# Two transformer blocks on one core: the low halves of a projection's input made by GpSimd in place of VectorE

## The chip, the cores and the metric

The kernel runs on one core of a Trainium2 chip. The metric is the device time of one execution in microseconds; the median of three runs is given. "TensorE", "VectorE", "ScalarE", "GpSimd" and "SyncE" are PE, DVE, ACT, POOL and SP in the profile.

## The reference

The input is x of 512 tokens by 1024 features. It goes through a first block (an RMS norm, an input projection, a mixer of sparse, convolutional, stick-breaking and dilated attention, group norms, an output projection, an RMS norm and a gated feed-forward) and then through four layers of a second kind. Each of these four is

```python
h = x * (1 + scale[0]) + shift[0]
y = mixer(h, w_in, ..., w_out)      # mLSTM, sliding window, HGRN2, differential attention
x = layer_norm(alpha * x + (1 + gate[0]) * y, ln_g[i, 0], ln_b[i, 0])
h = x * (1 + scale[1]) + shift[1]
y = (silu(h @ w_gate) * (h @ w_up)) @ w_down
x = layer_norm(alpha * x + (1 + gate[1]) * y, ln_g[i, 1], ln_b[i, 1])
```

All is fp32. What matters here are the matrix products h @ w. The kernel splits both factors in a high part, rounded to the engine's fast fp32r format, and a low part, the difference, and adds three products: hi x hi, hi x lo and lo x hi.

## The kernel before, in words

**Layout.** x lies in SBUF as eight chunks of 128 features by 512 tokens (`x[:, c, :]`). A product's input stands in `h_hi` and `h_lo`, eight chunks each. It comes from `h_tmp` (norms) or from `proj` (a mixer's output); there is one pair `h_hi`, `h_lo` for all of them.

**Weights.** They stream as 501 slots of 128 x 1024 through a ring of four (`RING`). SyncE loads a slot in `raw`, ScalarE copies it to `w_hi` (line 1187), GpSimd subtracts and writes `w_lo` (line 568), TensorE multiplies and counts `slot_used`, which lets ScalarE make the slot four further on. Four slots are always prepared ahead.

**Hand-over.** At each of 15 places a new input is produced while TensorE already starts on it: 5 in front of an input projection (the first block, layers 0 to 3), 5 in front of an output projection, 5 in front of a feed-forward. There TensorE runs `early_chunk(c)` for c = 0 to 7 on the first three slots (`EARLY`): it waits for `part_hi` of the chunk, does six matmuls on `h_hi`, waits for `part_lo`, and does three on `h_lo` (lines 753, 754, 758). Behind the eighth chunk the three slots are given free together; TensorE still has the fourth, prepared slot, some 5.4 us of work (24 matmuls, lines 665 to 667).

**Who makes the input.** ScalarE writes `h_hi` (line 1219, or 1266 with the scale and shift of a layer norm). VectorE writes `h_lo = value - h_hi` (`low`, line 1572). In a layer norm VectorE does, for each chunk, `times` (line 1617, x times a bank) and `less` (line 1621, x minus a bank); ScalarE then writes `h_hi` (1266) and `h_tmp` (1268), and VectorE subtracts (1572). ScalarE afterwards scales x eight times (line 1272), and goes on with its own program: in a feed-forward a Silu (line 1463, with a table load), then `w_hi` of the next slots. VectorE's order in this place is fixed by the code: `less(c)` stands behind the low half of an earlier chunk.

**Around it.** In the input projections of layers 1 and 3 VectorE copies finished banks to `proj` (line 1664). After the fourth tile it makes the rope tables (lines 1928 to 1941: on `rope_t`, no bank), and only afterwards the next copies; TensorE has four banks to fill meanwhile. GpSimd, beside `w_lo`, loads the positions for them (line 631) and, in layer 1, clears `swa_k` and `swa_v`.

**Queues.** Every engine runs its instructions in the order of its program; between engines there are semaphores. GpSimd's program before is `low_to(...)`, a loop over weight slots, with the first block's convolution, the DMA of positions, two memsets and parts of two mixers between.

Of the kernel before, what the change touches and what calls it, by code (L numbers as in the profile page):

```python
# [8 lines left out]
F32 = mybir.dt.float32  # L9
# [3 lines left out]
ALU = mybir.AluOpType  # L13
# [13 lines left out]
LEAD = 4  # L27
# [179 lines left out]
def stream_length(parts):  # L207
    n = 0
    for part in parts:
        tiles, values = IN_PROJ[part]  # L210
        n += len(tiles) + len(values) + n_gates(part) + (8 if part == "first" else 0) + DT + 2 * FT + 3 * DT
    return n


def program(nc, xT, wstream, ada, cond, cols, kept, bigc, layerc, pos, yT, parts):
    slots_total = stream_length(parts)
    ctx = ExitStack()
    with ctx:
# [345 lines left out]
        @block.gpsimd  # L564
        def _(pool):
            def low(k, i=0, step=0):
                pool.wait_ge(sm.hi_done, k + 1 + step * i)
                nc.gpsimd.tensor_tensor(w_lo[k % RING][:, :, :], raw[k % RING][:, :, :],  # L568
                                        w_hi[k % RING][:, :, :].bitcast(F32), ALU.subtract).then_inc(sm.lo_done, 1)

            def low_to(end):

                k, count = n["slot"], end - n["slot"]
                if count >= RING:
                    with loop(pool, count // RING) as i:
                        for q in range(RING):
                            low(k + q, i, RING)
                for q in range(count // RING * RING, count):
                    low(k + q)
                n.add(slot=count)  # L580

            def hgrn():

                pool.wait_ge(sm.hg_ready, 1)
                for s, step in enumerate(HG_STEPS):
                    for hd, lv in step:
                        if lv < 2:
                            continue
                        b = HG_WIDTH[lv - 1]
                        pool.wait_ge(sm.hg_mm, HG_MM[hd, lv - 1])  # L590
                        early, factor = halves(hg_k[:, hd, :], b)[0], hg_factor(hd, b, 1)
                        if lv == 9:
                            early, factor = early[:, 0:1, :], factor[:, 0:1, :]
                        nc.gpsimd.tensor_tensor(early, early, factor, ALU.mult).then_inc(sm.hg_early, 1)
                    if s in HG_LOW:
                        low(n["slot"])
                        n.add(slot=1)

            n = Counts()
            def gated_convolution():  # L600

                g = nc.gpsimd
                steps = 0

                def link(ins):

                    nonlocal steps
                    steps += 1
                    ins.then_inc(sm.conv_step, 1)
                    pool.wait_ge(sm.conv_step, steps)  # L610

                pool.wait_ge(sm.lin_free, len(IN_PROJ["first"][0]))
                for t in range(2):
                    u, y, w = proj[:, 13 + t, :], proj[:, 11 + t, :], [col("conv_w", 3 * t + i) for i in range(3)]
                    link(g.tensor_tensor(u, u, y, ALU.mult))
                    link(g.tensor_scalar(y, u, w[2], None, ALU.mult))
                    for lag in (1, 2):
                        link(g.tensor_scalar(conv_tmp[:, lag:S], u[:, 0:S - lag], w[2 - lag], None, ALU.mult))
                        link(g.tensor_tensor(y[:, lag:S], y[:, lag:S], conv_tmp[:, lag:S], ALU.add))
                    link(g.tensor_tensor(proj[:, 2 + t, :], y, proj[:, 2 + t, :], ALU.mult))  # L620

            first_slot = 0
            for at, part in enumerate(parts):
                tiles, values = IN_PROJ[part]
                if part == "first":
                    low_to(len(tiles) + len(values) + 8 + LEAD)
                    gated_convolution()
                if part in (1, 3):
                    low_to(first_slot + LEAD)
                    pool.wait_ge(sm.lin_free, lin_total(parts[:at]))  # L630
                    pool.dma_start(rope_i[:, :], pos).then_inc(sm.pos_loaded, 16)
                if part == 3:
                    low_to(first_slot + len(tiles) + len(values) + LEAD)
                    for hd in range(8):
                        pool.wait_ge(sm.rope_out, len(SWA_TILES) + 8 + hd + 1)
                        k = proj[:, 8 + hd, :]
                        nc.gpsimd.tensor_scalar(df_k[:, hd, :], k, block64[:, HD:HD + 1], float(HD), ALU.mult,
                                                ALU.mult).then_inc(sm.df_moved, 1)
                        pool.wait_ge(sm.df_moved, hd + 1)
                        nc.gpsimd.tensor_scalar(k, k, block64[:, 0:1], float(HD), ALU.mult,  # L640
                                                ALU.mult).then_inc(sm.df_keys, 1)
                if part == 1:
                    low_to(first_slot + LEAD + 2)
                    nc.gpsimd.memset(swa_k[:, :, :, :], 0.0)
                    op = nc.gpsimd.memset(swa_v[:, :, :, :, :], 0.0)
                    op.then_inc(sm.swa_zero, 1)
                if part == 2:
                    low_to(first_slot + len(tiles) + len(values) + LEAD)
                    hgrn()
                first_slot += stream_length([part])  # L650
            low_to(slots_total)

# [905 lines left out]
        def _(dve):  # L1558
# [25 lines left out]
                op.then_inc(sm.n_inv, 1)  # L1584
                dve.wait_ge(sm.n_spread, n["root"])

            def rms_input(gain):
                root()
                for c in range(DT + 1):
                    if c < DT:  # L1590
                        v.scalar_tensor_tensor(h_tmp[:, c, :], x[:, c, :], col(gain, c), inverse_root, ALU.mult,
                                               ALU.mult).then_inc(sm.h_ready, 1)
                    if c:
                        low(c - 1, h_tmp[:, c - 1, :])
                n.add(h=DT)

            def modulated_input(layer):

                for c in range(DT + 1):
                    if c:  # L1600
                        low(c - 1, h_tmp[:, c - 1, :])
                    if c < DT:
                        v.tensor_scalar(h_tmp[:, c, :], x[:, c, :], mod_col(layer, 0, ONE_SCALE, c),
                                        mod_col(layer, 0, SHIFT, c), ALU.mult, ALU.add).then_inc(sm.h_ready, 1)
                n.add(h=DT)

            def ln_columns(layer, sub, gain_at):

# [14 lines left out]
            def layer_norm(split):  # L1623
# [9 lines left out]
                dve.wait_ge(sm.ln_inv, 2 * n["ln"] - 1)  # L1633
                v.scalar_tensor_tensor(ln_drop, ln_mean, 1.0 / D, ln_rstd, ALU.mult, ALU.mult).then_inc(sm.ln_inv, 1)

                def part_low(c):
                    if split:
                        dve.wait_ge(sm.h_ready, n["h"] + c + 1)
                        low(c, h_tmp[:, c, :])

                dve.wait_ge(sm.ln_spread, 2 * n["ln"] - 1)
                for c in range(DT):
                    times(c)
                    if c == 0:
                        dve.wait_ge(sm.ln_spread, 2 * n["ln"])
                    if c == 1:
                        part_low(0)
                    less(c)
                    if c > 1:
                        part_low(c - 1)  # L1650
                part_low(DT - 1)
                n.add(h=DT if split else 0)

            def tile_done(slots):

# [112 lines left out]

            def group_norms(items):

                done = 0
                group_inverse(0)
                for t in range(len(items) + 1):
                    if t == 2 and len(items) > 4:
                        group_inverse(1)
                    if t < len(items):
                        group_norm(items, t, (4, 5))
                    if t:
                        for _ in items[t - 1]["src"]:
                            low(done, proj[:, done, :])  # L1780
                            done += 1
                n.add(gn=len(items))

            def attention(jobs, bufs):
                a, g = n["att"], n["att_g"]
# [379 lines left out]
            for at, part in enumerate(parts):  # L2165
# [1 line left out]
                layer = None if part == "first" else part  # L2167
                n.add(lc=2 if part == "first" else 1)
                if part == "first":
                    rms_input("g_mix")  # L2170
# [34 lines left out]
                if out_norms(part):  # L2205
                    group_norms(out_norms(part))
                else:
                    for c in range(DT):
                        low(c, proj[:, c, :])
                ahead = parts[at + 1] if at + 1 < len(parts) else None  # L2210
                if part == "first":
                    add_residual(1)
                    rms_input("g_ffn")
                    ffn(ahead, layer)
                    add_residual(3)
                else:
# [115 lines left out]
```

## Time and profile before

| what | value |
|---|---|
| time, median of 3 runs | 3532.15 us (3524.84 to 3534.9) |
| span of the profiled execution (its own time outside the span is not listed) | 3519.8 us |
| busy: TensorE / VectorE / ScalarE / GpSimd | 94% / 48% / 35% / 37% |
| mean granted TensorE clock | 0.964 of full speed |
| `w_lo` on GpSimd (line 568) | 501 x 2449 ns |
| `w_hi` on ScalarE (line 1187) | 501 x 1057 ns |
| DMA | 376.09 MB, 107 GB/s on average |

A line of the timeline gives the start in us, the duration in us, the engine, the line of the kernel, the operation, output<-inputs, the shape and how many instructions are merged in it. In brackets stands how long the engine was idle before, and which instruction of which engine ended that. A matmul's listed duration reaches past the start of the next one, since they are pipelined.

### The profile page before, as it was taken

The page shows a single profiled execution, that of the slowest core. Times are in us where ns is not written, and L with a number is a line of the kernel's source. Part 1 is how long each engine was busy: PE and PEld are TensorE (multiplying, and loading weights), DVE is VectorE, ACT ScalarE, POOL GpSimd, SP SyncE. Part 2 cuts the span into 40 slices and gives each one's busy share as a digit, 9 for nine tenths or more (in the row PEclk, how much of TensorE's full clock was granted, in tenths as well). Part 3 has the DMA queues.
Part 4 walks back from the last instruction along what each step waited for, and adds up shares of the span by engine and source line. Part 5 has one row for each costly group of instructions (what it writes and reads, how often), then busy time and mean ns, then how long its engine had stood idle before and what let it go on. Part 6 is the DMA issues. An engine that isn't in the chain of part 4 may idle for free.

```text
span 3519.8 us, 42555 instructions
## 1 busy us (share of the span) xinstructions
PE 3325.5 (94%) x14988; PEld 2629.1 (75%) x14988; DVE 1691.7 (48%) x2835; ACT 1230.2 (35%) x1914; POOL 1312.6 (37%) x603
## 2 busy tenths in 40 slices
PE   7987899999989999989999999999999998999998
PEld 6755578886757888767788878767888775678886
DVE  2344545512246554477655333666653447662223
ACT  3246433322335332336532243125332422643322
POOL 3430144443313444331444444533444343034442
PEclk9978999999999999989999999999999998999998
DMA  4310045532213554220455333103554231023331
GB/s 143 102 42 1 25 148 195 206 115 89 78 42 103 203 195 156 93 66 19 146 196 203 125 96 95 37 31 107 203 191 155 93 102 43 1 61 107 95 102 66
DMA packets 103105, 376.09 MB, mean 107 GB/s; under 512 B 11456, under 2 KB 11584, under 8 KB 102848
## 3 DMA queue, kind: packets, MB, share of 16 engines
q1 hardware_dynamic: 102816, 373.86, 32.0%
q8 instruction: 80, 1.31, 0.2%
q14 instruction: 49, 0.40, 0.0%
q0 software_dynamic: 160, 0.52, 0.0%
HBM read 372.24 MB, written 2.10 MB: 106 GB/s over the span
## 4 chain that ended last, share of the span: by engine, by line
PE 51%; issue 36%; POOL 10%; DVE 1%; ACT 1%; DMA 0%; POOLq 0%; SPq 0%; DVEq 0%; ACTq 0%
PE bank L665 14%; PE bank L667 14%; PE bank L666 14%; POOL w_lo L568 9%; PE bank L1096 1%; PE bank L709 1%; PE bank L710 1%; PE bank L711 1%; PE bank L1065 0%; PE bank L753 0%; PE bank L754 0%; PE bank L758 0%; PE bank L1003 0%; PE bank L1005 0%; PE bank L1004 0%
## 5 line engine op out<-in xcount | busy, mean ns | idle before, releaser
L568 POOL TENSOR_TENSOR w_lo<-raw,w_hi 128x1024 fp32r<-128x1024 f32 x501 | 1224.3, 2449 | 2100.7 <-ACT w_hi L1187 2100.7
L1187 ACT ACTIVATE w_hi<-raw 128x1024 fp32r<-128x1024 f32 x501 | 526.1, 1057 | 1234.8 <-PE bank L667 1021.2
L665 PE MATMUL bank<-h_hi,w_hi 128*128 128x512 f32 x2264 | 885.8, 391 | 12.0 <-DVE proj L1664 6.2
L666 PE MATMUL bank<-h_lo,w_hi 128*128 128x512 f32 x2264 | 882.5, 390 | 0.0
L667 PE MATMUL bank<-h_hi,w_lo 128*128 128x512 f32 x2264 | 882.1, 390 | 0.0
L665 PEld LDWEIGHTS bank<-h_hi,w_hi 128*128 128x128 f32 x2264 | 425.9, 188 | 106.0 <-POOL w_lo L568 8.2
L666 PEld LDWEIGHTS bank<-h_lo,w_hi 128*128 128x128 f32 x2264 | 426.0, 188 | 89.0 <-issue 1.0
L667 PEld LDWEIGHTS bank<-h_hi,w_lo 128*128 128x128 f32 x2264 | 426.0, 188 | 88.8
L2120 DVE CUSTOM_DVE_ANT_0 ada_raw<-ada_raw,cond_row 128x1024 f32<-128x1024 f32 x192 | 307.4, 1604 | 272.9 <-DMA ada_raw<-ada 263.1
L665 PE MATMUL bank<-hid_hi,w_hi 128*128 128x512 f32 x880 | 344.0, 391 | 0.0
L667 PE MATMUL bank<-hid_hi,w_lo 128*128 128x512 f32 x880 | 342.4, 389 | 0.0
L666 PE MATMUL bank<-hid_lo,w_hi 128*128 128x512 f32 x880 | 342.4, 389 | 0.0
L2136 DVE TENSOR_TENSOR hid_lo<-layer_const,hid_hi 128x512 f32 (+1 forms) x110 | 222.0, 2018 | 108.3 <-ACT hid_hi L1468 108.3
L1703 DVE SCALAR_TENSOR_TENSOR x<-bank,mod,x 128x512 f32<-128x512 f32 x64 | 48.0, 750 | 304.8 <-PE bank L667 294.7
L666 PEld LDWEIGHTS bank<-hid_lo,w_hi 128*128 128x128 f32 x880 | 165.2, 188 | 35.2 <-issue 1.0
L665 PEld LDWEIGHTS bank<-hid_hi,w_hi 128*128 128x128 f32 x880 | 165.2, 188 | 35.0 <-issue 1.0
L667 PEld LDWEIGHTS bank<-hid_hi,w_lo 128*128 128x128 f32 x880 | 165.2, 188 | 34.4
L1463 ACT ACTIVATE layer_const<-bank 128x512 f32<-128x512 f32 x110 | 65.6, 597 | 317.6 <-PE bank L667 308.5
L753 PE MATMUL bank<-h_hi,w_hi 128*128 128x512 f32 x360 | 154.7, 430 | 17.8 <-ACT h_hi L1266 11.5
L2133 DVE TENSOR_TENSOR layer_const<-bank,layer_const 128x512 f32<-128x512 f32 x110 | 75.9, 690 | 192.6 <-PE bank L667 163.2
L754 PE MATMUL bank<-h_hi,w_lo 128*128 128x512 f32 x360 | 149.9, 416 | 0.0
L1664 DVE COPY proj<-bank 128x512 f32<-128x512 f32 x68 | 45.5, 689 | 214.9 <-PE bank L667 204.1
(343 smaller groups left out, 4123.1 us busy)
## 6 DMA issues: line engine op xcount, KB each, us to landing
raw<-weights SPq DMA_DIRECT2D x501, 512.0 KB, 3.5
ada_raw<-ada SPq DMA_DIRECT2D x192, 512.0 KB, 4.3
layer_const<-layer_const SPq DMA_DIRECT2D x5, 512.0 KB, 4.4
x<-x_t SPq DMA_DIRECT2D x1, 2048.0 KB, 7.6
cond_row<-cond SPq DMA_DIRECT2D x4, 512.0 KB, 4.4
y_t<-x SPq DMA_DIRECT2D x8, 256.0 KB, 2.0
tables<-big_const SPq DMA_DIRECT2D x1, 768.0 KB, 7.5
cols<-columns SPq DMA_DIRECT2D x1, 569.5 KB, 8.6
```

The lines of the kernel that those rows point to most:

```text
L568: nc.gpsimd.tensor_tensor(w_lo[k % RING][:, :, :], raw[k % RING][:, :, :], w_hi[k % RING][:, :, :].bitcast(F32), ALU.subtract).then_inc(sm ...
L665: mm(out, w_hi[r][:, at, :], hi, start=first and at == 0, stop=False)
L666: mm(out, w_hi[r][:, at, :], lo, start=False, stop=False)
L667: op = mm(out, w_lo[r][:, at, :], hi, start=False, stop=last and at == len(pairs) - 1)
L753: mm(out, w_hi[r][:, c, :], h_hi[:, c, :], start=c == 0, stop=False)
L754: mm(out, w_lo[r][:, c, :], h_hi[:, c, :], start=False, stop=False)
L1187: fn(w_hi[t % RING][:, :, :], raw[t % RING][:, :, :], ACT.Copy).then_inc(sm.hi_done, 1)
L1463: fn(sil[q % 2], bank[(mt + 2 * q) % 4][:, :], ACT.Silu).then_inc(sm.sil_done, 1)
L1703: op = v.scalar_tensor_tensor(x[:, m, :], b[:, :], mod_col(layer, sub, ONE_GATE, m), x[:, m, :], ALU.mult, ALU.add)
L2120: v.tensor_tensor_reduce(w, w, cond_row[:, :], 1.0, 0.0, ALU.mult, ALU.add, ada_part[:, kc:kc + 1]).then_inc(sm.ada_used, 1)
L2133: v.tensor_tensor(sil[q % 2], bank[(mt + 2 * q + 1) % 4][:, :], sil[q % 2], ALU.mult).then_inc(sm.lin_free, 2)
L2136: v.tensor_tensor(hid_lo[:, q + 4 * i, :], sil[q % 2], hid_hi[:, q + 4 * i, :].bitcast(F32), ALU.subtract).then_inc(sm.part_lo, 1)
```

## The change

GpSimd gets a function `input_low` with the subtraction, which waits for `h_ready` (h_tmp is written, where it comes from a norm) and for `part_hi`. It is called in each part of the program in front of the input projection (but for the first), of the output projection and of the feed-forward. VectorE's low halves go in the same places; `part_lo` is now counted up by GpSimd there, and by VectorE in the first hand-over and for the feed-forward's hidden values.

```diff
+            def input_low(tile, scaled):
+                for c in range(DT):
+                    if scaled:
+                        pool.wait_ge(sm.h_ready, n["h"] + c + 1)
+                    pool.wait_ge(sm.part_hi, n["part"] + c + 1)
+                    nc.gpsimd.tensor_tensor(h_lo[:, c, :], tile(c), h_hi[:, c, :].bitcast(F32),
+                                            ALU.subtract).then_inc(sm.part_lo, 1)
+                n.add(part=DT, h=DT if scaled else 0)
...
                 if part == "first":
-                    low_to(len(tiles) + len(values) + 8 + LEAD)
+                    n.add(part=DT, h=DT)
+                    low_to(inputs + LEAD)
                     gated_convolution()
+                else:
+                    low_to(first_slot + LEAD)
+                    input_low(lambda c: h_tmp[:, c, :], True)
                 if part in (1, 3):
-                    low_to(first_slot + LEAD)
                     pool.wait_ge(sm.lin_free, lin_total(parts[:at]))
                     pool.dma_start(rope_i[:, :], pos).then_inc(sm.pos_loaded, 16)
...
+                low_to(first_slot + inputs + LEAD)
+                input_low(lambda c: proj[:, c, :], False)
+                low_to(first_slot + inputs + DT + LEAD)
+                input_low(lambda c: h_tmp[:, c, :], True)
+                n.add(part=FT)
...
             def modulated_input(layer):
-                for c in range(DT + 1):
-                    if c:
-                        low(c - 1, h_tmp[:, c - 1, :])
-                    if c < DT:
-                        v.tensor_scalar(h_tmp[:, c, :], x[:, c, :], ...).then_inc(sm.h_ready, 1)
+                for c in range(DT):
+                    v.tensor_scalar(h_tmp[:, c, :], x[:, c, :], ...).then_inc(sm.h_ready, 1)
...
                 for c in range(DT):
                     times(c)
                     if c == 0:
                         dve.wait_ge(sm.ln_spread, 2 * n["ln"])
-                    if c == 1:
-                        part_low(0)
                     less(c)
-                    if c > 1:
-                        part_low(c - 1)
-                part_low(DT - 1)
```

The same lines go from the group norms, from `rms_input` in front of the first block's feed-forward, and from the end of layer 1's mixer.

On VectorE, a layer norm in front of a feed-forward (`L1617` is `times`, `L1621` is `less`, `L1572` the low half, from the first chunk), before:

```order
618 L1617 TENSOR_TENSOR x<-x,bank 128x512
619 L1621 TENSOR_TENSOR x<-x,bank 128x512
620 L1617 TENSOR_TENSOR x<-x,bank 128x512
621 L1572 TENSOR_TENSOR h_lo<-h_tmp,h_hi 128x512
622 L1621 TENSOR_TENSOR x<-x,bank 128x512
623 L1617 TENSOR_TENSOR x<-x,bank 128x512
624 L1621 TENSOR_TENSOR x<-x,bank 128x512
625 L1572 TENSOR_TENSOR h_lo<-h_tmp,h_hi 128x512
```

The same place now (`L1633` is `times`, `L1637` is `less`):

```order
575 L1633 TENSOR_TENSOR x<-x,bank 128x512
576 L1637 TENSOR_TENSOR x<-x,bank 128x512
577 L1633 TENSOR_TENSOR x<-x,bank 128x512
578 L1637 TENSOR_TENSOR x<-x,bank 128x512
579 L1633 TENSOR_TENSOR x<-x,bank 128x512
```

`less` of the second chunk stood behind a low half, which itself stood behind `h_tmp` of ScalarE; now it follows `times` at once.

On GpSimd, the input projection of layer 1 (the loop above is the weight slots of layer 0; the slots' buffers have numbers), before:

```order
44 L568 TENSOR_TENSOR w_lo_64<-raw_56,w_hi_60 128x1024
45 L195 REGISTER_ALU
46 L195 COMPARE_AND_BRANCH
47 L631 DMA rope_i<-positions 128x512
48 L568 TENSOR_TENSOR w_lo_65<-raw_57,w_hi_61 128x1024
49 L568 TENSOR_TENSOR w_lo_62<-raw_54,w_hi_58 128x1024
50 L644 MEMSET swa_k 128x2048
51 L645 MEMSET swa_v 128x2048
```

The same place now:

```order
93 L568 TENSOR_TENSOR w_lo_64<-raw_56,w_hi_60 128x1024
94 L195 REGISTER_ALU
95 L195 COMPARE_AND_BRANCH
96 L605 TENSOR_TENSOR h_lo<-h_tmp,h_hi 128x512 x8
97 L645 DMA rope_i<-positions 128x512
98 L568 TENSOR_TENSOR w_lo_65<-raw_57,w_hi_61 128x1024
99 L568 TENSOR_TENSOR w_lo_62<-raw_54,w_hi_58 128x1024
100 L658 MEMSET swa_k 128x2048
101 L659 MEMSET swa_v 128x2048
```

Eight subtractions stand between the last weight slot that is prepared ahead and the DMA of the positions; the two slots and the memsets behind follow in the same order.

## Rows read from the trace of the kernel before

**Rows 1.** The page, its first line.

```profile
span 3519.8 us, 42555 instructions
```

**Rows 2.** Groups of instructions by shape: xcount | busy us, mean ns | idle before.

```profile
L1572 DVE TENSOR_TENSOR h_lo<-h_tmp,h_hi 128x512 fp32r<-128x512 f32 x80 | 56.4, 706 | 21.5 <-ACT h_tmp L1268 15.7 <-ACT h_hi L1219 5.6
...
L568 POOL TENSOR_TENSOR w_lo<-raw,w_hi 128x1024 fp32r<-128x1024 f32 x501 | 1224.3, 2449 | 2100.7 <-ACT w_hi L1187 2100.7
...
L615 POOL TENSOR_TENSOR proj<-proj 128x512 f32<-128x512 f32 x2 | 2.5, 1264 | 0.1
```

**Rows 3.** Waits of TensorE: waiter <- releaser: us in total, times, longest us.

```profile
PE bank L665 <- DVE proj L1664: 6.2, 2, 5.6
...
PE bank L665 <- POOL w_lo L568: 5.8, 5, 1.7
```

**Rows 4.** Timeline of ScalarE, layer norm in front of layer 1.

```profile
1477.17 0.81 ACT L1266 ACTIVATE h_hi<-x,ln_cols 128x512 fp32r<-128x512 f32 x1 [2.05 <-DVE x L1621]
...
1480.04 0.81 ACT L1266 ACTIVATE h_hi<-x,ln_cols 128x512 fp32r<-128x512 f32 x1 [1.36 <-DVE x L1621]
...
1481.47 0.80 ACT L1266 ACTIVATE h_hi<-x,ln_cols 128x512 fp32r<-128x512 f32 x1
...
1491.33 0.82 ACT L1266 ACTIVATE h_hi<-x,ln_cols 128x512 fp32r<-128x512 f32 x1 [0.40 <-DVE x L1621]
```

**Rows 5.** The same place on VectorE.

```profile
1478.72 0.69 DVE L1572 TENSOR_TENSOR h_lo<-h_tmp,h_hi 128x512 fp32r<-128x512 f32 x1 [0.99 <-ACT h_tmp L1268]
1479.33 0.68 DVE L1621 TENSOR_TENSOR x<-x,bank 128x512 f32<-128x512 f32 x1
```

**Rows 6.** The same place on TensorE: chunk 0, chunks 6 and 7.

```profile
1480.76 1.48 PE L758 MATMUL bank<-h_lo,w_hi 128*128 128x512 f32 x3
...
1494.45 0.84 PE L758 MATMUL bank<-h_lo,w_hi 128*128 128x512 f32 x3
...
1496.49 0.84 PE L758 MATMUL bank<-h_lo,w_hi 128*128 128x512 f32 x3
```

**Rows 7.** Timeline in front of the feed-forward of layer 0, ScalarE and TensorE.

```profile
1120.52 5.75 ACT L1272 ACTIVATE x<-x,ln_cols 128x512 f32<-128x512 f32 x8
...
1131.64 0.50 PE L665 MATMUL bank<-h_hi,w_hi 128*128 128x512 f32 x1 [1.04 <-POOL w_lo L568]
```

**Rows 8.** Timeline in front of the first block's feed-forward, ScalarE and TensorE.

```profile
473.00 1.28 ACT L1463 ACT_TABLE_LOAD   x1
...
482.91 0.84 PE L758 MATMUL bank<-h_lo,w_hi 128*128 128x512 f32 x3
483.33 0.60 ACT L1463 ACTIVATE layer_const<-bank 128x512 f32<-128x512 f32 x1 [9.04 <-PE bank L758]
```

**Rows 9.** Timeline of layer 1's rope tables: ScalarE, VectorE, GpSimd.

```profile
1498.40 1.04 ACT L1187 ACTIVATE w_hi<-raw 128x1024 fp32r<-128x1024 f32 x1
...
1507.76 10.21 POOL L568 TENSOR_TENSOR w_lo<-raw,w_hi 128x1024 fp32r<-128x1024 f32 x4
...
1513.69 1.06 ACT L1187 ACTIVATE w_hi<-raw 128x1024 fp32r<-128x1024 f32 x1 [4.38 <-PE bank L667]
...
1515.76 2.50 DVE L1935 TENSOR_SCALAR rope_t<-rope_t 128x512 f32<-128x512 f32 x1
...
1525.70 2.34 POOL L568 TENSOR_TENSOR w_lo<-raw,w_hi 128x1024 fp32r<-128x1024 f32 x1 [3.01 <-ACT w_hi L1187]
1525.72 2.88 DVE L1938 SCALAR_TENSOR_TENSOR rope_t<-rope_t,rope_t 128x512 f32<-128x512 f32 x1
...
1529.09 0.43 DVE L1941 TENSOR_SCALAR rope_t<-rope_t 128x512 f32<-128x512 f32 x1
```

**Rows 10.** Busy time by stretch; the number behind POOL's is the granted TensorE clock.

```profile
1530.20:1534.60 4.40, 4.40 (x10) 3.43 (x11) 1.71 (x3) 0.00 (x0) 0.00 (x0) 0.50 0.19 78
```

**Rows 11.** Timeline in front of layer 0, VectorE and TensorE.

```profile
828.47 2.09 DVE L1572 TENSOR_TENSOR h_lo<-h_tmp,h_hi 128x512 fp32r<-128x512 f32 x1 [0.70 <-ACT h_hi L1219]
...
830.62 0.96 PE L758 MATMUL bank<-h_lo,w_hi 128*128 128x512 f32 x3 [0.47 <-DVE h_lo L1572]
```

**Rows 12.** The page, costliest groups: VectorE in the feed-forwards.

```profile
L2136 DVE TENSOR_TENSOR hid_lo<-layer_const,hid_hi 128x512 f32 (+1 forms) x110 | 222.0, 2018 | 108.3 <-ACT hid_hi L1468 108.3
...
L2133 DVE TENSOR_TENSOR layer_const<-bank,layer_const 128x512 f32<-128x512 f32 x110 | 75.9, 690 | 192.6 <-PE bank L667 163.2 <-ACT layer_const L1463 29.4
```

More of the change, by code:

```diff
@@ L624, in _ @@
                 tiles, values = IN_PROJ[part]
+                inputs = len(tiles) + len(values) + n_gates(part) + (8 if part == "first" else 0)
                 if part == "first":
-                    low_to(len(tiles) + len(values) + 8 + LEAD)
+                    n.add(part=DT, h=DT)
+                    low_to(inputs + LEAD)
                     gated_convolution()
+                else:
+                    low_to(first_slot + LEAD)
+                    input_low(lambda c: h_tmp[:, c, :], True)
                 if part in (1, 3):
-                    low_to(first_slot + LEAD)
                     pool.wait_ge(sm.lin_free, lin_total(parts[:at]))
@@ L1585, in root, with rms_input @@
                 dve.wait_ge(sm.n_spread, n["root"])
-            def rms_input(gain):
+            def rms_input(gain, split):
                 root()
@@ L1592, in rms_input @@
                                                ALU.mult).then_inc(sm.h_ready, 1)
-                    if c:
+                    if c and split:
                         low(c - 1, h_tmp[:, c - 1, :])
-                n.add(h=DT)
+                n.add(h=DT, part=0 if split else DT)
             def modulated_input(layer):
-                for c in range(DT + 1):
-                    if c:
-                        low(c - 1, h_tmp[:, c - 1, :])
-                    if c < DT:
-                        v.tensor_scalar(h_tmp[:, c, :], x[:, c, :], mod_col(layer, 0, ONE_SCALE, c),
-                                        mod_col(layer, 0, SHIFT, c), ALU.mult, ALU.add).then_inc(sm.h_ready, 1)
-                n.add(h=DT)
+                for c in range(DT):
+                    v.tensor_scalar(h_tmp[:, c, :], x[:, c, :], mod_col(layer, 0, ONE_SCALE, c),
+                                    mod_col(layer, 0, SHIFT, c), ALU.mult, ALU.add).then_inc(sm.h_ready, 1)
+                n.add(h=DT, part=DT)
             def ln_columns(layer, sub, gain_at):
@@ L1634, in layer_norm @@
                 v.scalar_tensor_tensor(ln_drop, ln_mean, 1.0 / D, ln_rstd, ALU.mult, ALU.mult).then_inc(sm.ln_inv, 1)
[L1636 to L1639, printed above, removed]
                 dve.wait_ge(sm.ln_spread, 2 * n["ln"] - 1)
@@ L1645, in layer_norm @@
                         dve.wait_ge(sm.ln_spread, 2 * n["ln"])
-                    if c == 1:
-                        part_low(0)
                     less(c)
-                    if c > 1:
-                        part_low(c - 1)
-                part_low(DT - 1)
-                n.add(h=DT if split else 0)
+                n.add(h=DT if split else 0, part=DT if split else 0)
             def tile_done(slots):
@@ L1769, in group_norms @@
             def group_norms(items):
-                done = 0
                 group_inverse(0)
-                for t in range(len(items) + 1):
+                for t in range(len(items)):
                     if t == 2 and len(items) > 4:
                         group_inverse(1)
[L1776 to L1782, printed above, removed]
+                    group_norm(items, t, (4, 5))
+                n.add(gn=len(items), part=DT)
             def attention(jobs, bufs):
@@ L2169, in _ @@
                 if part == "first":
-                    rms_input("g_mix")
+                    rms_input("g_mix", True)
                     dve.wait_ge(sm.gate_in, 1)
@@ L2207, in _ @@
                 else:
-                    for c in range(DT):
-                        low(c, proj[:, c, :])
+                    n.add(part=DT)
                 ahead = parts[at + 1] if at + 1 < len(parts) else None
@@ L2212, in _ @@
                     add_residual(1)
-                    rms_input("g_ffn")
+                    rms_input("g_ffn", False)
                     ffn(ahead, layer)
```

## The prediction

> **What bounds the kernel now.** I read the page first: TensorE is busy 94% of a span of 3519.8 us (the table above and [rows 1]). An engine that full can only win at places where it waits, so the second view is the list of waits of TensorE [rows 3]. Two of its entries touch the work that the change moves. TensorE waits 5.8 us in five places for `w_lo`, the low half of a weight slot that GpSimd makes (the longest 1.7), and 6.2 us in two places for VectorE to copy a bank to `proj` (5.6 and 0.6). The third view is the timeline of a hand-over from a layer norm to the next projection; the prediction is made there. The change touches 14 of the kernel's 15 hand-overs: 5 in front of an output projection, 5 in front of a feed-forward, 4 in front of an input projection. The very first keeps VectorE.
>
> **What is added and removed.** 14 x 8 = 112 subtractions leave VectorE and go to GpSimd. On VectorE one takes 706 ns; GpSimd has no such row, but a product of the same shape, two SBUF inputs and one output, took 1264 ns there [rows 2]. So VectorE loses 112 x 0.69 = 77 us and GpSimd gains 112 x 1.26 = 142 us. Neither is a time of the kernel. What counts is whether TensorE asks for `h_lo` before GpSimd has it, and who else is freed.
>
> **Can GpSimd keep up?** In a hand-over TensorE does nine matmuls per chunk; at full clock a chunk takes 1496.49 - 1494.45 = 2.04 us [rows 6]. GpSimd needs about 1.3, so after chunk 0 it stays ahead. Chunk 0 of a layer norm: ScalarE starts h_hi at 1477.17, and h_tmp is finished when VectorE starts its subtraction, at 1478.72 [rows 4, 5]. GpSimd would finish at 1478.72 + 0.05 + 1.26 = 1480.03; TensorE reached the matmuls on h_lo at 1480.76 [rows 6]. All seven layer-norm hand-overs have this shape: no cost. Bounds for an unseen operation: at 1.26 nothing, and at 2.45 (a whole weight slot, twice the size [rows 2]) each chunk would be 0.4 late. I take 1.26, the row of the same shape and kind. In front of output projections the spread matmuls lengthen TensorE's chunk, so there is more room.
>
> **Term 1: ScalarE comes free earlier.** VectorE runs two operations on x, then one low half, per chunk; ScalarE writes h_hi and h_tmp per chunk. ScalarE's own step, with VectorE not in its way, is 1481.47 - 1480.04 = 1.43 us per chunk [rows 4]. But it waited 1.36 us for VectorE before chunk 1, since VectorE stood idle 0.99 us at the low half of chunk 0 and did `less(1)` only afterwards (1479.33) [rows 4, 5]. Without the low halves VectorE needs about 1.32 per chunk (two operations of 0.68, the second waiting for the first), less than 1.43, so ScalarE becomes the slower of the two and still beats TensorE's 2.04. ScalarE then finishes its 16 writes at 1477.17 + 8 x 1.43 = 1488.6; before, the last pair began at 1491.33 and ended at 1492.8 [rows 4], so it is 4.1 us earlier. Behind them stand eight scalings of x (5.75 [rows 7]), in a feed-forward a table load (1.28 [rows 8]), a Silu, and only then the next weight's high half. In front of the feed-forward of layer 0 VectorE's delay so reached TensorE: it idled 1.04 us for `w_lo` and went on at 1131.64 [rows 7]. In front of the feed-forward of the first block, where ScalarE is not late, the table load ran ten microseconds ahead (473.00), and the Silu began at 483.33, 0.42 after TensorE started its last three early matmuls (482.91) [rows 8]. With 4.1 us back ScalarE is in that situation behind all seven layer norms that feed a projection. The longest wait was 1.7, so all five disappear: 5.8 us. A listed idle understates the loss, because a matmul is listed with 0.39 but the next begins 0.23 later; that adds 0.16 each. Sum 5.8 + 5 x 0.16 = 6.6 us.
>
> **Term 2: the rope tables.** In the input projection of layer 1 ScalarE began `w_hi` at 1498.40; not late, it would begin at 1496.49 + 0.42 = 1496.9 [rows 6, 8, 9]. GpSimd's work behind it (two weight slots, two memsets, four weight slots, a block without a gap) moves 1.4 us earlier with it, while VectorE's tables start when the fourth tile is done, as before. VectorE's operations there, on `rope_t` alone, are stretched by GpSimd: L1935 took 2.50 beside `w_lo`, and an operation of the same form, L1941, 0.43 alone, and L1938 took 2.88 because `w_lo` began at 1525.70, 0.02 before it [rows 9]. The Trainium skill says why ("SBUF — State Buffer", section "SBUF: two separate sides"): the port pair that the two engines share is locked for a whole instruction. Worked through with these durations: the four slots at 1507.76 took 10.21, so 2.55 each; three of them now end at about 1514.0, while the fourth needs a `w_hi` that ends at 1513.69 + 1.06 = 1514.75. In that gap L1935 goes through at 1514.3 in 0.43, where it began at 1515.76 and took 2.50. What follows keeps a lead of 0.8 to 2 us, L1938 is then no longer caught by the `w_lo` at 1525.70, and the last operation, L1941, starts 0.1 to 0.4 us ahead of it. VectorE then comes to the banks at about 1525.9 in place of 1529.09 + 0.43 = 1529.5, 3.6 us earlier. TensorE had restarted at half its clock, granted 0.50 for 4.4 us [rows 10], after 5.6 us of idleness; with 2 us idle I expect it to keep the clock, as it did behind the idle 1.04 at 1131.64, whose matmul is listed with 0.50 (at half clock three take 1.48 [rows 6], over 0.6 for one), and that is 4.4/2 = 2.2 more. Sum 5.8. If the last operation just misses the gap, only 1.1 is left of it. In layer 3 the same tables cost 0.6; this goes too, with its 0.16: 0.8.
>
> **Term 3: a loss in front of layer 0.** Here h_tmp comes from VectorE, and GpSimd is busy with a weight slot. VectorE's subtraction was held by it (2.09 in place of 0.69, so until about 829.9) and TensorE waited 0.47 [rows 11]. Now GpSimd can start chunk 0 at 830.1 to 830.6, the later time if VectorE's waiting modulation goes first, and ends at 831.4 to 831.9, against 828.47 + 2.09 = 830.56. TensorE is 0.8 to 1.3 later on h_lo; some of that comes back at chunk 1, where it waited for a high half that is now early. I take +0.5 us, between a full return (0) and none (1.3).
>
> **Others, at nothing.** The positions' DMA on GpSimd's queue moves behind eight subtractions; it then leaves at about 1488.6 + 1.3 = 1490, more than 10 us before the tables. In normed products VectorE's two-SBUF operations share the lock with GpSimd; there are two such hand-overs, layers 0 and 2, at worst one held step each, 2 x 1.26 = 2.5; I take nothing, since TensorE's spread matmuls give room. VectorE enters the feed-forward early and its condition products meet GpSimd's last chunks; chunk 7 would be ready at 1490 and is asked for at 1496.49, so they may be held for 6 us. GpSimd's weight slots are not delayed: its next one needs banks that TensorE frees only after the last chunk. If that cover failed, each slot would cost at most its 2.45.
>
> **Sum.** -6.6 - 5.8 - 0.8 + 0.5 = -12.7 us: the profiled span would be 3507.1. Only the span of that execution is shown, and the runs' median lies 12.35 above it; against the median, 3532.15 - 12.7 = 3519.5.
>
> **Rivals.** (A) The gap in the tables is missed. Phases of 0.1 us decide it, and the trace of before cannot. Sum -12.7 + 4.7 = -8: 3524. (B) Nothing measurable: ScalarE's lateness has another source. For it speaks that the freed engine is busy only 48% of the span; against it the 0.40 that ScalarE idled for VectorE before a later h_hi of a layer norm [rows 4]. With terms 1 and 2 at nothing the time is 3530 to 3533. The Trainium skill ("Perfetto Trace Analysis", section "Optimizing Scalar/DVE Operations") warns that moving work between these two engines "might not help". The stretched rows agree with its reason, but only for operations without a bank: in the feed-forward, beside the same weight slots, L2136 (two SBUF inputs) averages 2018 ns and L2133 (a bank and SBUF) 690 [rows 12]. The operations of a layer norm read a bank, as L2133 does. (C) Slower: GpSimd does not keep up. Its place is each chunk after the first; it decides from a step of 2.04 us. For it speak the 1264 against 706 ns, and the lock with products and modulations. At a step of 2.3 (1.26, plus waits, plus one held operation of VectorE each) TensorE loses 14 x 7 x 0.26 = 25 us, net +17 after term 1: 3549. Against it: only three hand-overs have such VectorE operations at all.
>
> **From cases to numbers.** A measurement of this kernel can tell 0.3%, 10.6 us, from no change. Forecast 0.50, A 0.22, B 0.18, C 0.10. The forecast passes 10.6 by little, so of its 0.50 I count 0.40 as faster and 0.10 as same; of A 0.06 is faster, 0.16 same. Together: faster 0.46, same 0.10 + 0.16 + 0.18 = 0.44, slower 0.10. Range 3513 to 3532: it holds the forecast, A and most of B.
>
> **What would show it.** Right: no wait of TensorE for `w_lo` behind a layer norm; `w_lo` starting about 1 us behind the early matmuls there; ScalarE writing h_hi every 1.43 us; GpSimd's `h_lo` at about 1.26; the wait of 5.6 down to about 2, without a stretch at clock 0.50 behind it. Wrong: waits of the h_lo matmuls on GpSimd beyond layer 0; a GpSimd step over 2 us; a rope wait of 4 us or more.

## The result, and the profile after

The changed kernel takes 3510.43 us (median of 4 runs, 3505.9 to 3514.07); the kernel before, beside it, 3530.91 (4 runs). The ratio is 0.9945, 95% interval 0.9933 to 0.9956. A second comparison, experiment e5 below, gave 0.9951 (0.9937 to 0.9964), with 24 runs of before at a median of 3528.92. By these two ratios the change saves 17.3 to 19.4 us. The forecast was 3519.5, with a range from 3513 to 3532: the direction was right, the forecast was 9.1 us too high, and the measured time lies 2.6 us below the range.

The page of the changed kernel, two lines, answering to [rows 1]:

```profile
span 3506.9 us, 42581 instructions
...
PE 3323.4 (95%) x14988; PEld 2627.9 (75%) x14988; DVE 1642.4 (47%) x2723; ACT 1226.1 (35%) x1914; POOL 1467.7 (42%) x715
```

The forecast for this span was 3507.1. That it was met almost exactly is partly luck, as will be seen.

The waits of TensorE on `proj`, answering to [rows 3]. There is no row for `w_lo` any more:

```profile
PE bank L684 <- DVE proj L1670: 2.0, 1, 2.0
```

GpSimd's new instructions by shape (xcount: shortest/median/longest ns, first and last start), answering to [rows 2]:

```profile
L605 POOL TENSOR_TENSOR h_lo<-h_tmp,h_hi x72: 1280/1297/2348, 465.0 to 3135.7; 128x512 fp32r<-128x512 f32 x72
L605 POOL TENSOR_TENSOR h_lo<-proj,h_hi x40: 1261/1287/1789, 402.6 to 3084.8; 128x512 fp32r<-128x512 f32 x40
```

I had taken 1.26. The layer norm in front of layer 1, ScalarE (four of its lines) and then GpSimd, answering to [rows 4]:

```profile
1477.86 0.81 ACT L1285 ACTIVATE h_hi<-x,ln_cols 128x512 fp32r<-128x512 f32 x1 [2.05 <-DVE x L1637]
...
1479.29 0.80 ACT L1285 ACTIVATE h_hi<-x,ln_cols 128x512 fp32r<-128x512 f32 x1
...
1487.76 0.80 ACT L1285 ACTIVATE h_hi<-x,ln_cols 128x512 fp32r<-128x512 f32 x1
...
1489.17 5.75 ACT L1291 ACTIVATE x<-x,ln_cols 128x512 f32<-128x512 f32 x8
```

```profile
1479.46 11.19 POOL L605 TENSOR_TENSOR h_lo<-h_tmp,h_hi 128x512 fp32r<-128x512 f32 x8 [1.22 <-ACT h_tmp L1287]
```

Before, ScalarE's scaling of x in this place:

```profile
1492.75 5.75 ACT L1272 ACTIVATE x<-x,ln_cols 128x512 f32<-128x512 f32 x8
```

From the first h_hi to the first scaling of x ScalarE now takes 11.31 us; before it was 1492.75 - 1477.17 = 15.58. The eight steps are 1.41 us each, with no wait for VectorE. GpSimd's eight take 1.40 each, as fast as ScalarE feeds them. In front of the feed-forward of layer 0, whose early matmuls end at 1127.1, answering to [rows 7] (ScalarE, then GpSimd):

```profile
1126.70 0.60 ACT L1482 ACTIVATE layer_const<-bank 128x512 f32<-128x512 f32 x1 [0.16 <-PE bank L777]
```

```profile
1128.33 5.22 POOL L568 TENSOR_TENSOR w_lo<-raw,w_hi 128x1024 fp32r<-128x1024 f32 x2 [5.72 <-ACT w_hi L1206]
```

The Silu now waits for TensorE and not TensorE for the weight. `w_lo` starts 1.2 us behind the early matmuls in all four feed-forwards behind a layer norm, where it started 4.0 to 4.7 behind them.

The rope tables, answering to [rows 9, 10]: VectorE, TensorE, and the busy time of two stretches.

```profile
1514.84 0.43 DVE L1935 TENSOR_SCALAR rope_t<-rope_t 128x512 f32<-128x512 f32 x1
...
1518.83 0.69 DVE L1938 SCALAR_TENSOR_TENSOR rope_t<-rope_t,rope_t 128x512 f32<-128x512 f32 x1
...
1525.99 0.43 DVE L1941 TENSOR_SCALAR rope_t<-rope_t 128x512 f32<-128x512 f32 x1
```

```profile
1527.08 0.50 PE L684 MATMUL bank<-h_hi,w_hi 128*128 128x512 f32 x1 [1.96 <-DVE proj L1670]
```

```profile
1526.00:1530.00 4.00, 2.92 (x10) 2.38 (x11) 2.81 (x5) 2.65 (x4) 2.39 (x1) 0.83 0.21 64
1530.00:1534.00 4.00, 4.00 (x14) 3.19 (x14) 0.00 (x0) 0.00 (x0) 0.00 (x0) 0.75 0.37 129
```

L1935 slipped through the gap, and the wait fell from 5.64 to 1.96. But a stretch at half clock is still there; at 0.83 and 0.75 over four microseconds each it is (0.17 + 0.25) x 4 / 0.5 = 3.4 us long. Before, it was 4.8 us (granted 0.50 from the restart at 1530.17 to 1534.95). Now it does not begin at the restart: the granted clock is 1.00 from 1527.08 to 1528.60 and 0.50 from there to 1531.90.

In front of layer 0, answering to [rows 11] (GpSimd, TensorE):

```profile
830.33 11.34 POOL L605 TENSOR_TENSOR h_lo<-h_tmp,h_hi 128x512 fp32r<-128x512 f32 x8
```

```profile
831.86 1.14 PE L777 MATMUL bank<-h_lo,w_hi 128*128 128x512 f32 x3
```

TensorE is 831.86 - 830.62 = 1.24 later in the program's time, of which 0.37 was there before the hand-over began: 0.87 later on chunk 0.

### The profile page after: what moved, and what is told of

Same layout as the page of the kernel before. It is cut to its first block, busy times and chain, and to the rows that moved or that the text cites. A ratio compares the mean times of both kernels' runs of the same rounds, so it can differ in the third digit from the quotient of the medians.

```text
span 3506.9 us, 42581 instructions
## 1 busy us (share of the span) xinstructions
PE 3323.4 (95%) x14988; PEld 2627.9 (75%) x14988; DVE 1642.4 (47%) x2723; ACT 1226.1 (35%) x1914; POOL 1467.7 (42%) x715
## 4 chain that ended last, share of the span: by engine, by line
PE 79%; issue 4%; DVE 4%; POOL 2%; ACT 1%; POOLq 0%; DVEq 0%; ACTq 0%
PE bank L684 19%; PE bank L686 19%; PE bank L685 19%; PE bank L772 2%; PE bank L773 2%; PE bank L777 2%; PE bank L886 2%; PE bank L906 2%; PE bank L1115 1%; POOL w_lo L568 1%; PE bank L894 1%; PE bank L728 1%; PE bank L730 1%; PE bank L729 1%; PE bank L861 1%
## 5 line engine op out<-in xcount | busy, mean ns | idle before, releaser
L686 PE MATMUL bank<-h_hi,w_lo 128*128 128x512 f32 x2264 | 882.0, 390 | 0.0
L605 POOL TENSOR_TENSOR h_lo<-proj,h_hi 128x512 fp32r<-128x512 f32 x40 | 56.6, 1432 | 436.6 <-ACT h_hi L1238 436.6
```

Of the source, the lines that this page charges most:

```text
L686: op = mm(out, w_lo[r][:, at, :], hi, start=False, stop=last and at == len(pairs) - 1)
```

## The experiments

Each was timed beside the kernel before. Where an edit is written against the changed kernel, `MOVED` is the set of hand-overs that GpSimd serves.

**e1_again: the kernel before once more.** No edit but line numbers.

> VectorE makes all low halves, as before: the same instructions on every engine in the same order as the kernel before. Theory (the profiled execution of before was a lucky one of its kind; the others lose more at the same hand-overs): ratio 1.000, but a profiled span above 3519.8, between 3522 and 3533, with the extra in longer stretches at half clock and not in new waits. Rival (the profiled execution was typical and 10 us lie outside the span): span 3519 to 3521 again.

Ratio 1.0003 (0.9995 to 1.0012), span 3527.2. The program is the same, the span 7.4 us longer. The sum of TensorE's listed waits is the same in both (179.4 and 179.3 us). Two pieces of the layer 0 stage, first in the trace of before and then in this one:

```profile
828.50:831.90 3.40, 2.77 (x10) 1.69 (x11) 2.71 (x3) 1.30 (x3) 1.52 (x1) 1.00 0.37 111
...
1033.30:1036.70 3.40, 3.40 (x9) 0.55 (x8) 0.00 (x0) 2.39 (x5) 0.00 (x0) 1.00 0.00 0
```

```profile
832.40:835.80 3.40, 3.40 (x8) 2.72 (x9) 2.70 (x3) 1.32 (x3) 1.49 (x1) 0.51 0.38 111
...
1037.20:1040.60 3.40, 2.97 (x5) 0.72 (x6) 0.00 (x0) 1.52 (x3) 0.00 (x0) 0.51 0.00 0
```

The same matmuls at the same place had the full clock in one execution and 0.51 in the other. Added up over the trace, TensorE was granted 0.50 for 251 us in before and for 268 here: 17 / 2 = 8.5 us of work. The theory holds in its main point, that the extra is half clock and not waits. Most of it does not lie at the hand-overs behind layer norms: 10 of the 17 us are in the layer 0 stage and 7 in the first block's first stage.

**e2_norms and e3_others: which hand-overs carry the gain.**

```diff
-MOVED = ('ln_ffn', 'ln_in', 'mod', 'out', 'rms_ffn')
+MOVED = ('ln_ffn', 'ln_in')            # e2_norms
+MOVED = ('mod', 'out', 'rms_ffn')      # e3_others
```

> Only the seven layer norms that feed a projection hand their low halves to GpSimd; VectorE keeps the other seven hand-overs that the change moves (layer 0's input, the first feed-forward, five output projections). Theory (ScalarE comes free earlier behind a layer norm, and that is all of the gain): about the whole difference, ratio 0.994 (span 13 to 20 us below the kernel before), TensorE never waits for w_lo. Rival (every hand-over gives a part of it, as half of the subtractions stay): ratio 0.997.

> The complement: layer 0's input, the first feed-forward and the five output projections go to GpSimd; the seven layer norms keep VectorE. Theory: nothing but the loss before layer 0, +0.5 us, so ratio 1.000 (0.999 to 1.001), and TensorE still waits 5 to 7 us for w_lo and 5 to 6 us for the tables' banks. Rival (every hand-over gives a part): ratio 0.997.

e2: 0.9952 (0.9939 to 0.9965), no wait for `w_lo`. e3: 1.0004 (0.9995 to 1.0013). Seven hand-overs carry everything, seven nothing. In e3 the wait for `w_lo` was larger than foretold, with a ScalarE as late as before; the early matmuls ended sooner (see term 1 below):

```profile
PE bank L688 <- POOL w_lo L569: 8.9, 6, 2.4
...
PE bank L688 <- DVE proj L1689: 6.8, 2, 5.9
```

**e4_first: VectorE keeps the low halves, later.** Only the order within a layer norm changes, against before:

```diff
-                    if c == 1:
-                        part_low(0)
                     less(c)
-                    if c > 1:
-                        part_low(c - 1)
-                part_low(DT - 1)
+                    if c >= 2:
+                        part_low(c - 2)
+                for c in range(DT - 2, DT):
+                    part_low(c)
```

> VectorE keeps all low halves, but in a layer norm it makes the low half of chunk c behind the second operation on chunk c+2, so that ScalarE is not held by it at chunk 1. Theory (what counts is the pace of ScalarE, not which engine makes low halves): VectorE now needs 2 x 0.68 + 0.69 = 2.05 us per chunk, as TensorE does, so ScalarE is held from then on by VectorE's three operations; it starts chunk 1 earlier by 0.7 to 1.3 us but the pace of 2.05 gives that back: ScalarE ends at 1477.2 + 7 x 2.05 + 1.4 = 1493, no earlier than before. Ratio 1.000, waits for w_lo of about 6 us remain. Rival (only the stall at chunk 1 mattered): ScalarE 1.4 us earlier throughout, w_lo waits down to 0 to 2 us, ratio 0.997.

0.9971 (0.9959 to 0.9982): my theory's number fell, the rival's stood. ScalarE, from chunk 0 (the last line begins at the first scaling of x):

```profile
1478.64 0.81 ACT L1289 ACTIVATE h_hi<-x,ln_cols 128x512 fp32r<-128x512 f32 x1 [1.73 <-DVE x L1645]
...
1480.06 0.80 ACT L1289 ACTIVATE h_hi<-x,ln_cols 128x512 fp32r<-128x512 f32 x1
...
1483.20 0.82 ACT L1289 ACTIVATE h_hi<-x,ln_cols 128x512 fp32r<-128x512 f32 x1 [0.23 <-DVE x L1645]
...
1485.12 0.82 ACT L1289 ACTIVATE h_hi<-x,ln_cols 128x512 fp32r<-128x512 f32 x1 [0.40 <-DVE x L1645]
...
1492.31 2.21 ACT L1295 ACTIVATE x<-x,ln_cols 128x512 f32<-128x512 f32 x3
```

Its step is 1.92, as before, not my 2.05; so the stall at chunk 1 is saved for good, and 13.67 us pass until the scaling instead of 15.58. Those 1.9 us take all but 0.3 us of the waits for `w_lo` away; the wait at the tables is 4.5, because there the last operation just missed the gap between two weight slots (0.43 alone, 2.50 here):

```profile
1526.44 2.50 DVE L1965 TENSOR_SCALAR rope_t<-rope_t 128x512 f32<-128x512 f32 x1
```

By the ratios, 10.2 of the 17.3 to 19.4 us are so had without giving GpSimd anything.

**e5_after: the changed kernel in more executions.** No edit but line numbers.

> The changed kernel itself again, in more executions. Theory (the profiled execution of before was at the fast edge, and the gain is 17 to 20 us): ratio 0.9945, median 3510 to 3511, spans 3502 to 3512. Rival (the gain is the 12.7 of the sum, and the first comparison was high by chance): ratio 0.9964, median 3516 to 3518.

0.9951 (0.9937 to 0.9964), median 3510.68, span 3507.2. The rival's 0.9964 is the very end of this interval and outside the first one (to 0.9956); the theory's 0.9945 is inside both.

**e6_ffn and e7_in: the two kinds of layer norm apart.** `MOVED = ('ln_ffn',)` and `MOVED = ('ln_in',)`.

> Only the four layer norms in front of a feed-forward hand their low halves to GpSimd. Theory (each of the two kinds of place has its own gain): the four waits of TensorE for w_lo there (1.0, 1.4, 1.5, 1.7 and 0.16 each) vanish, the waits for the tables' banks (5.6 and 0.6) stay: -6.3 us in direct terms, ratio 0.997 to 0.998. Rival (one place carries it all): ratio 0.9995 or 0.995.

> Only the three layer norms in front of an input projection (layers 1 to 3) hand their low halves to GpSimd. Theory: the wait for the tables' banks falls from 5.6 to 2.0 and that of layer 3 from 0.6 to 0, the four waits for w_lo in front of feed-forwards stay: -5.8 - 0.8 - 0.35 = -7 us, ratio 0.998 to 0.997. Rival (as in the run before): ratio 0.9995 or 0.995.

e6: 0.9967 (0.9955 to 0.9979), 11.6 us. e7: 0.9984 (0.9975 to 0.9993), 5.6 us. Together 17.3, as the whole change in e5 (each interval is 3 to 4 us to either side). The waits split as foretold. Of e6, with no row for `w_lo`:

```profile
PE bank L688 <- DVE proj L1689: 6.3, 2, 5.9
```

Of e7:

```profile
PE bank L688 <- POOL w_lo L569: 7.0, 4, 2.3
...
PE bank L688 <- DVE proj L1689: 2.0, 1, 2.0
```

But the feed-forwards are worth 11.6, not 6.3.

**e8_late and e9_dose: ScalarE made late again.** Against the changed kernel, with k = 5 and k = 2; `link` waits until the instruction has ended:

```diff
+                    for _ in range(k if c == DT - 1 else 0):
+                        link(fn(h_tmp[:, c, :], x[:, c, :], ACT.Identity,
+                                bias=ln_col(H_SHIFT, c), scale=ln_col(H_SCALE, c)))
                     fn(h_tmp[:, c, :], x[:, c, :], ACT.Identity, bias=ln_col(H_SHIFT, c),
```

> The changed kernel, but behind a layer norm ScalarE writes the last chunk's h_tmp six times in place of once (the value is the same), so that it is 5 x 0.8 to 5 x 0.9 = 4.0 to 4.5 us late for the scalings of x and the next w_hi, as it was before the change. GpSimd still makes all low halves; only chunk 7's comes later, and it is not asked for by then. Theory (ScalarE's lateness is the whole cause): the waits of TensorE for w_lo (5 to 7 us in five places) and for the tables' banks (5 to 6 us) return, ratio 0.999 to 1.000. Rival (the relief of VectorE itself gives part of the gain, for instance at the tables or by an earlier start of other work): ratio 0.996 to 0.998.

> The changed kernel with ScalarE writing the last chunk's h_tmp three times in place of once behind a layer norm (the same value), which makes it 2 x 0.84 = 1.7 us later; of the 4.1 us won 2.4 are left. Theory (a wait returns only when ScalarE is later than the wait was long): as the kernel with the low half made two chunks later, which left 1.9 us: waits for w_lo 0 to 1 us in all, wait for the tables' banks 3 to 4.5, ratio 0.996 to 0.9975. Rival (each microsecond of ScalarE's lateness counts, in proportion): waits for w_lo of 2 to 3 us, ratio 0.998.

e8: 1.0009 (1.0000 to 1.0018). GpSimd still makes all low halves, VectorE is as free as in the changed kernel, and the whole gain is gone. The waits are back:

```profile
PE bank L688 <- POOL w_lo L569: 8.0, 5, 2.2
...
PE bank L688 <- DVE proj L1692: 6.4, 2, 5.9
```

e9: 0.9941 (0.9927 to 0.9954), no loss at all. The theory's rule (a threshold) holds here and the rival's proportion does not, but I had put the threshold too low: `w_lo` starts 2.2 to 2.7 us behind the early matmuls in the feed-forwards, and TensorE does not wait for it there; from 3.9 on it did. Between them lie e4's two feed-forwards in layers 2 and 1: 3.05 behind, no wait; 3.31 behind, a wait of 0.31. Beyond 3.0 each microsecond counts in full: 4.04 behind cost 1.04 (before), 5.17 cost 2.13 (e1). Both rules so hold, each on its side of 3.0. The one row for `w_lo` left in e9's waits (1.6 us, and the same in e10) is another place, TensorE's first early matmul in front of the last feed-forward, where the other traces list 1.6 to 1.8 us for `h_hi`. In front of the input projections `w_hi` still begins at its earliest, 0.42 before the early matmuls end, and the tables' wait stays 2.0 where I expected 3 or more.

**e10_memset, e11_memset_before, e12_best: the rest at the tables.** In part 1 of GpSimd's program:

```diff
                 if part in (1, 3):
                     low_to(first_slot + LEAD)
+                    if part == 1:
+                        nc.gpsimd.memset(swa_k[:, :, :, :], 0.0)
+                        op = nc.gpsimd.memset(swa_v[:, :, :, :, :], 0.0)
+                        op.then_inc(sm.swa_zero, 1)
                     pool.wait_ge(sm.lin_free, lin_total(parts[:at]))
...
-                if part == 1:
-                    low_to(first_slot + LEAD + 2)
-                    nc.gpsimd.memset(swa_k[:, :, :, :], 0.0)
-                    op = nc.gpsimd.memset(swa_v[:, :, :, :, :], 0.0)
-                    op.then_inc(sm.swa_zero, 1)
```

e11 makes the same move in the kernel before; e12 is e10 with `mod` taken out of `MOVED`.

> The changed kernel with layer 1's two memsets (1.80 us each), which stand on GpSimd between two weight slots beside the first operations of the rope tables, moved to directly behind the last low half of that hand-over, where GpSimd is idle for 7 us. Theory (the tables are late because GpSimd's block without a gap holds VectorE): VectorE is 2 to 3.6 us earlier, the wait of 2.0 for the tables' banks vanishes: 2.0 + 0.16, and up to 1.7 of half clock: -2 to -4 us against the changed kernel, ratio against before 0.994. Rival (only the weight slots behind the memsets set the pace of the tables): the wait stays at 2, ratio 0.995.

> The kernel before (VectorE makes all low halves) with the same move of the two memsets; in program order they stand behind the weight slots made ahead, so they run before or within the layer norm. Theory: the wait for the tables' banks falls from 5.6 to 0 to 2, the five waits for w_lo stay at 6 to 8 us; -3.6 to -6 us, ratio 0.9985. Rival: the memsets hold a low half of VectorE in the layer norm for up to 3.6 us, which TensorE then waits for: ratio 1.000 with a new wait there.

> The changed kernel with the memsets moved and with layer 0's input left to VectorE. Theory: -0.5 us more than the memsets alone, by the hand-over in front of layer 0, whose early matmuls end 0.3 to 0.6 us sooner; ratio against before 0.994, no loss anywhere. Rival: the hand-over in front of layer 0 costs nothing on either engine, same time as with the memsets alone.

e10: 0.9934 (0.9920 to 0.9947), median 3505.96, span 3501.7. The memsets now run in GpSimd's idle time (first fence). The wait of 2.0 is gone, and the clock stays at 1.00 where it had fallen (second fence, the last column but two):

```profile
1492.29 1.81 POOL L650 MEMSET swa_k<- 128x2048 f32 x1
1494.04 1.81 POOL L651 MEMSET swa_v<- 128x2048 f32 x1
```

```profile
1524.00:1530.00 6.00, 6.00 (x29) 4.95 (x28) 3.55 (x5) 3.19 (x4) 2.96 (x2) 1.00 0.29 89
```

The stage from layer 1's first early matmul to that of its output projection takes 156.7 us; in the changed kernel 160.5, in before 166.2. e11: 0.9974 (0.9964 to 0.9984): the wait of 5.6 is gone (the stage takes 157.3; 0.5 of waiting for `proj` is left, in layer 3), the waits for `w_lo` stay (7.0 in five). By the ratio that is 9.2 us where I gave at most 6 (the interval begins at 5.6): the wait went altogether, and the half clock with it. e12: 0.9938 (0.9923 to 0.9952), not to be told from e10; the early matmuls in front of layer 0 take 17.85 us in it and 18.24 in e10, 0.4 less. The fastest of all by its median is e10. Against the changed kernel only its stage shows the gain (3.8 us); the intervals of the totals overlap.

## Why the forecast was right and where it failed

**Chunks in time, GpSimd's pace: right.** 1.29 and 1.30 us by median, fed every 1.4, against 2.04 that TensorE needs. Rival C did not happen; e3 has the places where the lock might have hurt, and lost nothing measurable. Its price was also added up wrong in the prediction: 25.5 less term 1's 6.6 is 18.9, not 17; nothing else hangs on it.

**Term 1, the mechanism: right.** ScalarE's end, 4.3 us earlier (foretold 4.1), is the whole cause. e8 gives it back and loses everything; e2 and e3 put it at the layer norms. Rival B is out.

**Term 1, the size: this step failed.** I counted 6.6 us, of which 6.25 in front of feed-forwards. They are worth 11.6 in e6. The stages, from a hand-over's first early matmul to the next one's, the last one to ScalarE's last operation (mean of the traces, and extremes), show where it lies. Late: before, e1, e3, e7, e8, e11 for feed-forwards; before, e1, e3, e6, e8 for layer 1's input. Not late: after, e2, e5, e9 for both, with e6, e10, e12 for feed-forwards and e7 for the input. Left out are e4, which lies between, and for the input the three kernels in which the memsets moved.

```
stage                      ScalarE late           not late               difference  foretold
feed-forward, layer 0      373.0 (372.2 to 374.7)  370.1 (369.7 to 370.6)   -2.9       -1.2
feed-forward, layer 1      372.5 (371.7 to 373.2)  370.1 (369.9 to 370.6)   -2.4       -1.5
feed-forward, layer 2      372.3 (371.7 to 373.3)  370.1 (369.8 to 370.4)   -2.2       -1.7
feed-forward, layer 3, end 383.2 (382.6 to 383.8)  379.2 (378.9 to 379.4)   -4.0       -1.8
input of layer 1           165.3 (164.7 to 166.2)  160.5 (159.9 to 161.0)   -4.8       -5.8
```

The four feed-forwards sum to -11.5. Two things were missing. The waits for `w_lo` differ from execution to execution: at layer 0 they were 1.04, 1.05, 2.36, 0.93, 2.25 and 0.97 us in the six late traces. The early matmuls before them took 19.36, 19.36, 18.00, 19.47, 18.09 and 19.43 us, according to how long they ran at half clock; early matmuls and wait together are 20.3 to 20.4 us in every one of the 24 late cases. So ScalarE alone set when TensorE went on, and a short wait meant slow early matmuls, not a less late ScalarE. Over the four places their mean is 6.9, where the one execution I read had 5.6: with 4 x 0.16 that makes 7.5. And the sum had no term for the half clock in these stages: I took it to be the same with and without the wait. By the granted clock TensorE had 0.50 for 49.7 us over these four stages where ScalarE was late and 42.3 where it was not; half of the 7.4 is 3.7. Together 11.2. The largest piece of the half clock (4.0 of the 7.4) is in the last stage, and some of it at the very end, in a layer norm that the change does not touch. TensorE there in before, and the stretch's busy time:

```profile
3500.54 3.16 PE L796 MATMUL bank<-kept,sums_down 128*128 128x1 f32 x16 [1.50 <-DVE sums_down L1707]
```

```profile
3499.50:3504.00 4.50, 3.16 (x16) 3.07 (x16) 2.16 (x6) 0.60 (x1) 0.00 (x0) 0.67 0.00 0
```

and in the changed kernel:

```profile
3488.89 1.95 PE L815 MATMUL bank<-kept,sums_down 128*128 128x1 f32 x16 [1.50 <-DVE sums_down L1713]
```

```profile
3488.00:3491.00 3.00, 1.95 (x16) 1.86 (x16) 1.90 (x6) 0.60 (x1) 0.00 (x0) 1.00 0.00 0
```

The same 16 matmuls take 1.2 us less, because they fell into a stretch at full clock. It is no chance: in the six traces in which ScalarE is late in front of the feed-forwards they take 2.66 to 3.17, in the eight others 1.95 or 1.96. Why the earlier arrival spares them the half clock was not tried by itself and stays open.

**Term 2: right in kind, one piece too large.** Foretold were 5.8 at the tables: 3.6 of waiting, where 3.7 went, and 2.2 for a stretch at half clock that was to vanish. It only shrank from 4.8 to 3.4 us, which is 0.7: that TensorE would keep its clock after 2 us of idleness, as it did after 1.04, was wrong. The stage gives 4.8. Rival A, the missed gap, is what e4 shows (wait 4.5, stage 163.0), where ScalarE was only 0.4 us later than in the changed kernel. In layer 3 the wait of 0.6 went. e10 confirms what held VectorE: GpSimd's block beside the tables.

**Term 3: right.** The early matmuls in front of layer 0 take 18.2 to 18.4 us with GpSimd and 17.8 to 18.2 with VectorE: +0.4 by the means, foretold +0.5. It is too small to be seen in a total.

**From the span to the time: this step failed too.** I set the sum against the median of three runs and carried the 12.35 us between the span and that median along, as if they lay around the span. Only about 2 do (3508.96 - 3506.9 in the changed kernel, 3529.23 - 3527.2 in e1; 1.7 to 3.0 in all runs on record). The execution that I read so took about 3522 (an estimate: its own time is not on record); of 65 timed runs of the kernel before one was faster (3521.14), and their median is 3529.1. And the three runs' 3532.15 was itself 3.1 above this median. So the 9.1 us by which the forecast missed are 3.1 from the baseline and about 6 from a sum that was too small: 5.3 too little in front of the feed-forwards (of which the one execution that I read accounts for 1.3, its short waits), 1.0 too much at the tables, and the rest is within the interval of the gain, 4 us to either side. That the span was met within 0.2 us is luck: two errors cancelled. The sum was too small, and the execution of before was short by 7.4 us, since it lacked 17 us at half clock that e1, the same program, had. From e1 to the changed kernel the spans differ by 20.3. In all fourteen traces the span less the listed waits of TensorE less half of its time at 0.50 lies between 3212 and 3218: the rest of the program hardly changed.

## What to carry to other kernels

When an engine is relieved, look for who waited on it within the loop and what that one does next: here GpSimd's help paid only by ScalarE's earlier end, and e4 had about half of it or more by letting VectorE make each low half one chunk later. Slack of this kind is a threshold, so it is worth measuring how late the producer may be before anyone waits (here `w_lo` could start 3.05 us behind the early matmuls for nothing, and 3.31 cost the first 0.31). One profiled execution gives the mechanism but not the size: compare its own time with the spread of the timed runs before a sum is set against their median, and where the clock falls to half around the place, widen the range by what the stretch costs.

## What the runs showed of the hardware that I had not expected

The time that TensorE spends at a granted clock of 0.50 differs by 17 us between two executions of one program (251 and 268), in stretches as short as 3.4 us that are there in one trace and missing in the other. The spread of the 65 runs fits this: the fastest (3521.14) had a mean granted clock of 0.965 and the slowest (3538.33) of 0.960, and 0.005 of 3530 us is 17.6, where the times differ by 17.2. GpSimd's two-input subtraction of 128x512 took 1.26 us at least, and up to 2.35 in single cases; a series of eight in a layer norm ran at 1.40 each, beside VectorE's operations on a bank, which kept their 0.69.
